# Attention output finished in channel layout, without transposes of output rows

## The reference, cut to what matters

```python
logits = jnp.einsum('bqhgd,bqkhd->bqhgk', qg, k_sel) * (HEAD_DIM ** -0.5)
logits = jnp.where(valid[:, :, None, None, :], logits + bias, -jnp.inf)
p = jax.nn.softmax(logits, axis=-1)
o = jnp.einsum('bqhgk,bqkhd->bqhgd', p, v_sel)
# ... in sublayer:
y_a = (o * jax.nn.silu(g_attn)) @ w_attn_out
```

## Time and profile before

| what | value |
|---|---|
| median of the runs | 3389.51 us |
| the profiled execution | 3395.7 us, span 3394.0 us |
| TensorE, matmul busy | 3245.1 us, 96% |
| VectorE busy | 2697.9 us, 79% |
| ScalarE busy | 1467.3 us, 43% |
| GpSimd busy | 1038.4 us, 31% |
| mean granted TensorE clock | 0.984 |

### The profile page before, as it was taken

The page is one execution under the profiler, slowest core; times in us unless marked ns, Lnnn a source line. Parts: engine busy times, 40 slices in busy tenths (PEclk is TensorE's granted clock), DMA queues, the critical chain, the costliest instruction groups (busy, mean ns, idle before and its releaser), DMA issues. The chain is left out here.

```text
span 3394.0 us, 50403 instructions
## 1 busy us (share of the span) xinstructions
PE 3245.1 (96%) x19461; PEld 2999.2 (88%) x19461; DVE 2697.9 (79%) x4071; ACT 1467.3 (43%) x1961; POOL 1038.4 (31%) x888
## 2 busy tenths in 40 slices
PE   7999999999999999999998999999999989899998
PEld 4999888999999999999997887787777879899987
DVE  2542788898989999999995999999999965875444
ACT  2322566988930200001002776676767740432121
POOL 3222111543335300000002453444533324674200
PEclk9999998999999999999998999999999999999999
DMA  6465535445555643344445323223222245577343
GB/s 236 131 190 165 155 100 141 158 149 187 185 180 178 256 177 138 138 162 170 159 144 145 78 59 81 75 57 99 59 60 61 60 154 199 159 236 257 127 143 114
DMA packets 381524, 485.53 MB, mean 143 GB/s; under 512 B 49296, under 2 KB 304464, under 8 KB 379685
## 3 DMA queue, kind: packets, MB, share of 16 engines
q1 hardware_dynamic: 325605, 287.14, 28.2%
q10 hardware_dynamic: 44352, 149.49, 12.4%
q0 software_dynamic: 11392, 46.68, 3.5%
HBM read 301.98 MB, written 184.13 MB: 143 GB/s over the span
## 5 line engine op out<-in xcount | busy, mean ns | idle before, releaser
L1140 PE MATMUL psum<-ha,gt 128*128 128x352 f32 x8136 | 1352.8, 324 | 7.7 <-DVE ha L1414 4.4
L1140 PEld LDWEIGHTS psum<-ha,gt 128*128 128x128 f32 x8136 | 1323.0, 189 | 11.6 <-DVE ha L1414 4.7
L1450 DVE SCALAR_TENSOR_TENSOR cv<-cv,vecs,cv 128x1056 f32<-128x1056 f32 (+1 forms) x480 | 607.7, 1342 | 0.0
L1942 ACT CAST at<-psum 128x1024 fp32r<-128x1024 f32 (+2 forms) x308 | 289.5, 940 | 265.2 <-PE psum L1853 263.4
L2016 DVE TENSOR_TENSOR at<-psum,at 128x1024 fp32r<-128x1024 f32 (+2 forms) x308 | 346.7, 1126 | 6.3 <-ACT at L1942 5.8
L717 PE MATMUL psum<-br,br 128*128 128x352 f32 x2016 | 337.1, 328 | 15.0 <-DVE br L2389 10.5
L1853 PE MATMUL psum<-ident,at 128*128 128x128 f32 (+1 forms) x2320 | 344.6, 272 | 6.0 <-DVE at L2016 4.8
L717 PEld LDWEIGHTS psum<-br,br 128*128 128x128 f32 x2016 | 330.4, 190 | 19.4 <-issue 11.8
L1271 ACT ACTIVATE gt<-psum 128x1056 f32<-128x1056 f32 x80 | 84.0, 1050 | 600.3 <-PE psum L1140 600.3
L791 DVE TENSOR_SCALAR_CACHE_REDUCE gl<-gt,gl 128x1792 bf16<-128x1792 f32 (+8 forms) x263 | 337.7, 1350 | 1.2
L1872 PE MATMUL psum<-at,at 128*128 128x512 f32 (+1 forms) x1160 | 327.2, 391 | 7.4 <-ACT at L1950 7.3
(11 more groups left out here) (255 smaller groups left out, 4142.7 us busy)
## 6 DMA issues: line engine op xcount, KB each, us to landing
scratch_ws<-gt SPq DMA_DIRECT2D x112, 512.0 KB, 4.0
gt<-scratch_ws ACTq DMA_DIRECT2D x110, 512.0 KB, 5.0
gt<-in_w_in_dram SPq DMA_DIRECT2D x60, 512.0 KB, 5.8
scratch_gm<-gt ACTq DMA_DIRECT2D x32, 528.0 KB, 3.0
br<-scratch_gm ACTq DMA_DIRECT2D x32, 528.0 KB, 3.7
scratch_m<-br POOLq DMA_DIRECT2D x32, 528.0 KB, 5.1
at<-scratch_q SPq DMA_DIRECT2D x128, 128.0 KB, 2.9
scratch_u<-gl POOLq DMA_DIRECT2D x16, 528.0 KB, 4.2
```

What stands on the lines that cost most here:

```text
L1140: return nc.tensor.matmul(of[:, j, 0:W // 3], part[:, c, :], a[:, c, j * (W // 3):(j + 1) * (W // 3)], start=(c == 0 and k == 0), stop=(c ...
L1450: ins = nc.vector.scalar_tensor_tensor(to[:, 0:width], mine[:, k_:k_ + width], tap, to[:, 0:width], ALU.mult, ALU.add)
L1942: nc.scalar.copy(phi[j % 3][:, 0:len(mine), 0:n], turned[j % 2][:, 0:len(mine), 0:n]).then_inc(s_phi, 1)
```

## The change

The output stays in channel layout from the accumulator to the store. ScalarE copies the two halves of the accumulator apart with two copies, so that both come to lie on the same 64 partitions (the lower half for even units, the upper for odd ones). GpSimd adds them (`fold`, step last+3). The reciprocals of the sums, now taken at step first, are written to DRAM as one row per unit by SyncE, and read back spread over 64 partitions (step first+2). GpSimd multiplies the loaded gate by them in place (`gain`, step first+4). VectorE makes one product of folded output and scaled gate (`finish`, step last+5), and SyncE stores it. The transposes of output rows and their two places per unit in the ring are gone. Gates have four half-height slots in place of three. Near rows have four buffers in place of two, the plain copy is made for each head, and GpSimd's program follows the steps: a near row stands at the step in which the row four before it is consumed, and the queries of the next unit follow the unit's last near row.

The diff, cut to its core (declarations of tiles and semaphores are left out):

```diff
+    NEARS = 4
+    GATES = 4
...
-        self.rows_at = at([n + self.LAG + 1 for n in self.last])
-        self.cols_at = at([n + self.LAG + 2 for n in self.last])
+        self.total_at = at(self.first)
+        self.spread_at = at([n + 2 for n in self.first])
+        self.gain_at = at([n + 4 for n in self.first])
+        self.fold_at = at([n + self.LAG + 1 for n in self.last])
+        self.out_at = at([n + self.LAG + 3 for n in self.last])
...
+        for e in range(GROUP * count):
+            self.near_at[ends[e - self.NEARS] if e >= self.NEARS else self.begin].append((e // GROUP, e % GROUP))
...
+            def total_row(u):
+                n = plan.queries(u)
+                sp.wait_ge(s_total, u + 1)
+                sp.dma_start(scr["ri"][u, 0:GROUP * n].rearrange("(q h) -> q h", h=GROUP), rinv[0:n, u % 4, :]).then_inc(s_row[u % 2], 16)
+
+            def spread(u):
+                n = GROUP * plan.queries(u)
+                sp.wait_ge(s_row[u % 2], 16 * (u // 2 + 1))
+                if u >= 2:
+                    sp.wait_ge(s_gain, u - 1)
+                sp.dma_start(wide[side(u), 0:n], scr["ri"][u:u + 1, 0:n].to_broadcast([HD, n])).then_inc(s_wide[u % 2], 16)
...
+            def near_row(u, h):
...
+                if e >= plan.NEARS:
+                    pool.wait_ge(s_ring, plan.final(*divmod(e - plan.NEARS, GROUP)) + 1)
+                row = near[e % plan.NEARS]
+                if width > n:
+                    nc.gpsimd.tensor_copy(row[:, 0:width - n], mine[:, o:o + width - n])
+                nc.gpsimd.tensor_tensor(row[:, width - n:width], bias[g % 2][:, h, c0:c0 + n],
+                                        mine[:, o + width - n:o + width], ALU.add).then_inc(s_near, 1)
...
+            def gain(s, u):
...
+                nc.gpsimd.tensor_tensor(gate(u), gate(u), wide[side(u), 0:GROUP * n].rearrange("d (q h) -> d h q", h=GROUP),
+                                        ALU.mult).then_inc(s_gain, 1)
...
+            def fold(s, u):
...
+                pool.wait_ge(s_acc, 2 * (u + 1))
+                nc.gpsimd.tensor_tensor(folded(u), folded(u), acc_lo[side(u), 0:n], ALU.add).then_inc(s_fold, 1)
...
+            for s in plan.steps:
+                for u in plan.fold_at[s]:
+                    fold(s, u)
+                for u in plan.gain_at[s]:
+                    gain(s, u)
+                for u, h in plan.near_at[s]:
...
+                    near_row(u, h)
+                    if h == GROUP - 1 and u + 1 < len(units):
+                        queries(u + 1)
...
-                            pe.wait_ge(s_acc, u)
+                            pe.wait_ge(s_acc, 2 * u)
...
-                nc.scalar.copy(accs[u % 2][:, 0:n], acc[:, 0:n]).then_inc(s_acc, 1)
+                nc.scalar.copy(folded(u), acc[0:HD, 0:n]).then_inc(s_acc, 1)
+                nc.scalar.copy(acc_lo[side(u), 0:n], acc[low, 0:n]).then_inc(s_acc, 1)
...
+            def finish(u):
+                dve.wait_ge(s_gain, u + 1)
                 dve.wait_ge(s_fold, u + 1)
+                mine = folded(u).rearrange("d (h t) -> d h t", h=GROUP)
+                nc.vector.tensor_tensor(mine, mine, gate(u), ALU.mult).then_inc(s_out, 1)
```

More of the change, by code:

```diff
@@ L1521, in __init__ @@
         self.copy_at = at([n + self.LAG for n in self.last])
-        self.rows_at = at([n + self.LAG + 1 for n in self.last])
-        self.cols_at = at([n + self.LAG + 2 for n in self.last])
+        self.total_at = at(self.first)
[3 more added lines that the diff above has]
+        self.out_at = at([n + self.LAG + 3 for n in self.last])
         self.queries_at = at([self.last[u - 5] + 1 if u >= 5 else self.begin for u in range(count)])
         self.masks_at = at([done[u - 3] + 1 if u >= 3 else self.begin for u in range(count)])
-        self.gates_at = at([self.last[u - 3] + self.LAG + 3 if u >= 3 else self.begin for u in range(count)])
+        self.gates_at = at([self.last[u - 4] + self.LAG + 4 if u >= 4 else self.begin for u in range(count)])
         self.store_at = at([n + self.LAG + 3 for n in self.last])
+        final = {x[1:3]: x[0] for x in placed if x[3] == len(self.chunks(x[1])) - 1}
+        ends = [final[u, h] for u in range(count) for h in range(GROUP)]
+        self.near_at = {s: [] for s in self.steps}
+        for e in range(GROUP * count):
+            self.near_at[ends[e - self.NEARS] if e >= self.NEARS else self.begin].append((e // GROUP, e % GROUP))
+        self.folds_by = {s: sum(n + self.LAG + 1 <= s for n in self.last) for s in range(self.begin - 1, self.end)}
+        self.gains_by = {s: sum(n + 4 <= s for n in self.first) for s in range(self.begin - 1, self.end)}
+        self.nears_before = {s: sum(len(self.near_at[v]) for v in self.steps if v < s) for s in self.steps}
         per = len(self.TILES)
@@ L1533, in __init__ @@
         for s in self.steps:
-            for key in ([("max",) + x for x in self.chunks_at[s]] + [("rows", u) for u in self.rows_at[s]]
-                        + [("cols", u) for u in self.cols_at[s]]):
-                self.slot[key] = len(self.slot)
+            for x in self.chunks_at[s]:
+                self.slot[("max",) + x] = len(self.slot)
     def queries(self, u):
@@ L1598, in attention_stage @@
         phi, plo = parts[18:21], parts[21:24]
[L1599 to L1603, removed]
+        near = parts[24:24 + plan.NEARS]
+        acc_hi, acc_lo, wide = parts[28:31]
+        ga = parts[31:33]
+        least, total, rinv = parts[33:36]
+        room = parts[36]
         ktmp = nc.alloc_sbuf_tensor_at("at_ktmp", [P, FRONT], F32R, offset=mem.at["at4"])
-        ktmp0 = nc.alloc_sbuf_tensor_at("at_ktmp0", [P, KEYS], F32R, offset=mem.at["at38"])
+        ktmp0 = nc.alloc_sbuf_tensor_at("at_ktmp0", [P, KEYS], F32R, offset=mem.at["at36"])
         turned = [mem.psum[0][:, k * 1024:(k + 1) * 1024].rearrange("p (b n) -> p b n", b=2) for k in range(2)]
@@ L1616, in attention_stage, with side, gate, folded @@
         block = ctx.enter_context(nc.Block())
+        def side(u):
+            return slice((u % 2) * HD, (u % 2 + 1) * HD)
+        def gate(u):
+            return ga[u // 2 % 2][side(u), :, 0:plan.queries(u)]
+        def folded(u):
+            return acc_hi[side(u), 0:GROUP * plan.queries(u)]
         def bank(key):
@@ L1715, in _ @@
                         queries(u)
+                for u in plan.spread_at[s]:
+                    spread(u)
+                for u in plan.total_at[s]:
+                    total_row(u)
                 for u in plan.store_at[s]:
@@ L1786, in nears @@
                 o = keys_of(t)[1] - width
[L1787 to L1800, removed]
@@ L1875, in values @@
                     last.then_inc(s_pv, 1)
[L1877 to L1893, removed]
             pe.wait_ge(s_set, SET)
@@ L1910, in _ @@
                     scores(*todo.pop(0))
[L1911 to L1914, removed]
         @block.scalar
@@ L1975, in masked @@
                     dve.wait_ge(s_near, GROUP * u + h + 1)
-                    other = near[h % 2][0:n, 0:w]
+                    other = near[(GROUP * u + h) % plan.NEARS][0:n, 0:w]
                 else:
@@ L1984, in masked, with totals @@
                                                op0=ALU.add, op1=ALU.min, accum_out=least[0:n, u % 3, h, c:c + 1]).then_inc(s_ring, 1)
-            def rows(u):
+            def totals(u):
                 n = plan.queries(u)
[L1988 to L1995, removed]
-                dve.wait_ge(s_fold, u + 1)
[L1997 to L2006, removed]
+                dve.wait_ge(s_exp, GROUP * (u + 1))
+                if u >= 4:
+                    dve.wait_ge(s_row[u % 2], 16 * (u // 2 - 1))
+                nc.vector.reciprocal(rinv[0:n, u % 4, :], total[0:n, u % plan.SUMS, :]).then_inc(s_total, 1)
+            def finish(u):
+                dve.wait_ge(s_gain, u + 1)
+                dve.wait_ge(s_fold, u + 1)
+                mine = folded(u).rearrange("d (h t) -> d h t", h=GROUP)
+                nc.vector.tensor_tensor(mine, mine, gate(u), ALU.mult).then_inc(s_out, 1)
             for s in plan.steps:
@@ L2017, in _ @@
                                             phi[j % 3][:, 0:len(mine), 0:n].bitcast(F32), ALU.subtract).then_inc(s_plo, 1)
[L2018 to L2021, removed]
+                for u in plan.total_at[s]:
+                    totals(u)
+                for u in plan.out_at[s]:
+                    finish(u)
 def branch_stage(nc, mem, x, w, out, scr):
```

65 lines of the change are left out of this document (41 added, 24 removed).

## The result

The changed kernel takes 3371.63 us (median of five runs, 3368.22 to 3375.77). Against runs of the kernel before on the same chip the ratio is 0.9939, with a 95% interval of 0.9924 to 0.9954: faster by 0.6%, some 20 us, where 48 were forecast. The profiled execution has a span of 3369.9 us against 3394.0.

The account below looks back on a forecast made before the run. TensorE and VectorE, both nearly full and feeding each other, were taken to bound the 895.5 us attention stage. TensorE's terms gave 846 us, VectorE's 850.5 to 839; 847.5 was taken, 48 less, so 3341.5 us, range 3311 to 3386.

Parts of the forecast that it names:

- VectorE's part: Attention stage, VectorE: 105.9 us of fold, scaling and gating removed, 61 us of final product added, 45 us shed.
- the surcharge: VectorE's final product: 0.27 us on top of 0.68 undisturbed, scaled by GpSimd's busy share, 70% against 43%.
- The waits: TensorE in the attention stage: 19.5 us on row scaling gone, 11.0 on query halves mostly gone, 25 added for the copy.
- TensorE's removed work: Attention stage: six transposes fewer per unit at 0.109 us each, 44 us in all.
- TensorE's sum: Attention stage: 895.5 less 44 of transposes, 19.5 and 11 of waits, plus 25 for the copy, 846 us.
- the sum: Attention stage: the longer of TensorE's 846 us and VectorE's 850.5 to 839 taken as its length, 847.5, 48 less.
- the 25 us of the copy: Unit ends: TensorE's first value product waits for two ScalarE copies, not one; 25 us over 67, bounds 0 and 39.
- VectorE's 850: Attention stage: 895.5 less 45 us shed, 850.5 if VectorE's idle time stays; 839 if half its score waits go.
- Rival (a): VectorE's final product: GpSimd's lock on SBUF inputs makes it 1.32 us, the stage loses 18 us; 3371 us, chance 0.13.
- Rival (b): Attention stage: nothing measurable, removed work lay beside a loop closed elsewhere and waits move; 3389 us, chance 0.07.
- (d): Attention stage: TensorE's waits all vanish and the copies come early, stage 820 us; 3314 us, chance 0.08.
- Rival (c): Unit ends: ScalarE's second copy falls whole on 67 units and delays the transposed copy behind it; +39, 3428 us, chance 0.10.

Follow-up runs that it names:

- run e: The changed kernel without GpSimd's fold and gain, both ScalarE copies kept; ratio 0.9902 to the kernel before, stage 856.0 us.
- run f: The changed kernel with ScalarE's second copy reading a constant and TensorE waiting for the first copy alone; ratio 0.9878 to the kernel before, stage 850.7 us.
- run b: The changed kernel without ScalarE's second copy, low-part product left out of the output; ratio 0.9874 to the kernel before, stage 847.9 us.
- run j: The kernel of run b with two VectorE memsets of 272 ns behind each final product; ratio 0.9978 to the kernel before, stage 885.8 us.
- run g: The kernel of run b with five 128-column products more on TensorE where it had waited for the second copy; ratio 1.0008 to the kernel before, stage 895.1 us.
- run h: The changed kernel, whole, with both accumulator copies ahead of the exponentials on ScalarE; ratio 0.9910 to the kernel before, stage 865.0 us.

## Why the prediction was wrong

**VectorE's part held by rows.** The final product was forecast at 0.95 us and has 0.960. Its undisturbed part was right: of its 64 full instances the 22 that began with no GpSimd instruction under way have a mean of 0.683 us (0.68 was forecast), the other 42 have 1.104. That the surcharge came out as forecast is partly luck: scaled by GpSimd's busy share it would be 0.19 us in run e, where GpSimd is busy 50% of the stage, and it is 0.10 there (0.781 - 0.683), so the share alone doesn't set it. 105.9 us removed and 61.4 added are the forecast 45 by rows. By busy time in the stage it is 34 (831.1 to 797.2), since neighbours overlap: before, VectorE's instructions in the stage last 948 us together, in 831 us of busy time.

**The waits held.** 19.5 and 11.0 us went; the copy's wait rose by 25.3 us where 25 were forecast. GpSimd is at 622 us where 593 were forecast: the gain takes 1587 ns and not 1282, which is 20 of the 29 us.

**TensorE's removed work was mis-sized a little.** Six transposes were put at 44 us; its busy time fell by 35 (851.5 to 816.2), which leaves TensorE's sum 9 us short.

**The step that failed is the sum:** "The longer is between 846 and 850, so I take 847.5". It set two engines' sums side by side as if they ran apart and the longer one hid the other's terms. So the 25 us of the copy, booked on TensorE, vanished under VectorE's 850. The runs show the contrary: with TensorE freed from that wait the stage is 850.7 (run f), 847.9 without the copy (run b), VectorE's sum; with it 871.1. That the sum is met almost to the microsecond is partly luck: in run b VectorE's busy time is 36 us under that before and not 45, and its idle time 11 us under it, which the 850.5 left as it was. Each engine waits for the other many times a unit, and the reading that fits the runs is that a delay of either moves the next meeting: 37.0 us on VectorE cost 37.9 (run j), 61 on TensorE 47 (run g). With the 23 us that run b shows for the copy on top of VectorE's sum the stage would be 850 + 23 = 873, against 871.1 measured. These 23 us are known from the runs after it and no fixed price: with the copies ahead of the exponentials the wait fell by 28.5 us and the stage by 6 (run h).

TensorE's own sum missed the other side of this. Its waits on VectorE's low parts and ring banks rose from 4.8 to 21.2 us. -35 - 19.5 - 11 + 25 + 16 = -24 accounts for the 22.6 measured within 2 us; that is bookkeeping of one engine's busy and idle time, and does not say which term is the cause. The 9 us of transposes and the 16 us of waits are in run b as well (816.6 us busy, 21.2 us of such waits), at a stage of 847.9, so they do not lengthen it by themselves; what parts run b from the change is the copy. Why these waits rose no run isolates: they are 16 us or more in every kernel with the new output path except that of run g, whose TensorE has 61 us more to do (8 us), and under 5 in every one with the old.

**The rivals.** Rival (a) named 3371, which is the time, but not the cause: its final product of 1.32 us would have shown, and it was 0.96. GpSimd's fold and gain are worth 15 us of stage (run e), which the forecast had in its 0.27 us surcharge (17 us over 64 products). Rival (b) is out, since the ratio's interval lies below 1, and (d), since TensorE still waits 55 us. Rival (c) named the right place, and the sign that the prediction set for it was there: ScalarE's wait for TensorE shrank by 69 us and the copy became TensorE's largest wait by far. Its price is 23 us in the change and 12 in the kernel before, not 39, and it comes by TensorE's wait; the copy of probabilities behind it, which (c) counted in, costs about 3 (run f). So it did not outweigh the savings.

## What to carry to other kernels

Where two engines are both over 90% busy in a stage and meet at every step, don't take the longer of two sums: here a wait added on one came on top of the other's work, and a wait taken away was partly replaced by the next. Give an instruction that releases another engine's next product a price of its own at the place where it releases: here 37 us of added copies, on an engine with hundreds of us of idle time, cost 23 us of stage. And read a stage's length between the same two instructions beside the span, which carries along what varies ahead of the stage; where it and the ratio part, as for the two kernels with the moved half, more executions are needed.

## What was not expected of the hardware

GpSimd's gain on 64 x 512 reads one input with a stride of four elements and takes 1587 ns, where the fold with contiguous inputs takes 1289; that the stride is the cause was not tested by itself. ScalarE's copy of 64 partitions takes 574 to 582 ns, that of 128 partitions 575: half the partitions save nothing. A 128-column fp32 product of the identity stands in the trace as two matmul instructions and costs TensorE 0.18 us (61 us for 335); a transpose of the same width is one instruction and takes 0.109. The longest final product took 2209 ns, three times its undisturbed time of 0.683 us, with two GpSimd instructions under way one after the other. And the first copy of transposed probabilities began between 1851.7 and 1866.3 us in kernels that differ in the attention stage alone, a spread of 14.6 us that the span carries along.
